# A two-block transformer kernel on one core: roots of the first mixing by logarithms, seven banks for projections, another order for down banks and condition sums

## The chip, the cores and the metric

One core of one Trainium2 chip runs the whole program in one launch. The metric is device microseconds of one execution. The engines are TensorE (PE; its weight loads, PEld, overlap its matmuls), VectorE (DVE), ScalarE (ACT), GpSimd (POOL) and SyncE (SP, which here only issues DMAs). Each works through its own queue in order; semaphores tie them together.

## The reference

512 tokens of width 1024 go through a first block and then two layers of a second block, all in float32.

```python
# first block: three kinds of attention, a gated merge, a squared-relu MLP
aq, ak, bq, bk, cq, ksel, kwin = (rms_norm(...) per head of 64, with a gain)
oa = rms_norm(diff_attention(aq, ak, av, lam), subln) * 0.8          # att_a: two maps, p0 - lam * p1
ob = banded_attention(bq, bk, bv, window 128, sinks)                  # att_b
oc = nsa_attention(cq, compressed, selected, window; sigmoid gates)   # att_c
x = x + sum_n(sigmoid(mg_n) * (branch_n @ w_branch_n)) @ w_out
x = x + square(relu(rms_norm(x) @ w_up)) @ w_down
# each of two layers: mod = silu(c) @ w_ada + b_ada gives 9 vectors of 1024 (shift, scale, gate x 3)
x = x + 0.5 * gate0 * swiglu(modulate(rms_norm(x)))                   # width 2816
x = x + gate1 * mixer(modulate(rms_norm(x)))                          # chunked attention, pooling, forgetting attention
x = x + 0.5 * gate2 * swiglu(modulate(rms_norm(x)))
```

## The kernel before

**Matmuls.** Activations lie with features on partitions and the 512 tokens in the free dimension, as chunks of 128 features. Each float32 matmul of a projection is three in the faster fp32r form: high x high, high x low, low x high (L1536 to L1538). A *group* is one output tile of 128 features x 512 tokens: 8 chunks x 3 matmuls, in one bank of PSUM out of eight. POOL splits each weight piece of 512 KB into its high and low part (L1489, L1492) ahead of PE. In the feed-forward parts pairs of output tiles are computed as a *set* of 7 products per side with half-size operands (`new_set`, L942; matmuls L1605 to L1607). A product is 12 matmuls of 256 columns; the products come in the order P1, P2, P5, P6, P7, P3, P4, each for the gate side and then for the up side. P1 writes into `banks[1]` and P2 into `banks[0]` of its side, from `SET_BANKS`: ((6, 2), (7, 3)) or ((6, 4), (7, 5)). A set's first sums (L2112, L2114 on DVE) use banks 0 and 1, which hold silu(c) until the last condition sum has read them; ACT moves the weights there first (L1787).

**Queues.** `plan` (L1148) writes out one list of steps, and every engine walks through it, taking the steps that are its own; so the order of steps fixes the order of each queue. `HELD` notes for each bank which semaphore frees it, and `take(bank)` puts that wait ahead of the next writer. A group takes the next bank of its *ring*, a tuple of banks; `RING_AT` keeps the position per ring, also across stages. `late(step, quanta)` postpones a step by so many quanta of two chunks; `passed` gives out at most one per quantum.

**Roots.** Every normed projection (and each of the four outputs of att_a, "differential") needs 1/sqrt of a mean. `new_root` puts: ACT squares the bank (L1829); two quanta later PE sums over partitions into bank 4 (L1630); then there are two ways. With `logs` false, ACT takes a Sqrt (L1839) and DVE the reciprocal in two halves (L2162), at the third and fourth quantum. With `logs` true, ACT does Identity with scale and bias, Ln, Exp with -0.5, and a Square into the other buffer, for which it waits for the output of the root before (L1843 to L1850); DVE makes a correction step of two products (L2153, L2157). Both end in the output product (L2178, or L2172 with L2175 for att_a), which frees the group's bank. Before the change the layers' second projections (inside att_a2) use logarithms and all other roots a Sqrt.

**Tables.** ACT's functions come in table sets. A load (ACT_TABLE_LOAD) is put by the compiler ahead of an activation whose function the present set lacks. `put("tables")` loads the set with logarithm and exponential by hand.

**Attention.** `attend` gives four beats per *duo* (one or two blocks of queries of a pair of heads): turn and scores, exponentials, products with V, scaling of probabilities. `weave` puts the stage's dense groups between the beats. Scores use banks 0 and 1, transposes 2 and 3, sums 4, outputs 5. DVE takes minima (L2204) and inverses (L2218); in att_a it also joins the two maps (L2236), behind ACT's scaling (L1885), and only then are the score banks free. The first mixing has 12 duos in att_a with 13 dense groups, 16 in att_b with 4 groups and the compression.

**Condition sums.** `mod` is 144 rows of 1024 products, as 72 loads of 1 MB (issued by ACT) and 72 sums of two rows each on DVE (L2297), nine in each of eight runs of eight down groups (`with_ada`). A down group's result is added to x on DVE (L2458), which frees its bank. `ada_sum` steps stand ahead of the group that they are given to, and each issues the load two ahead.

Of the kernel before, what the change touches and what calls it, by code (L numbers as in the profile page):

```python
# [12 lines left out]
S = 512  # L13
# [16 lines left out]
ADA_PART = 9  # L30
# [19 lines left out]


SCORE_BANKS, T_BANKS, SUM_BANK, O_BANK = (0, 1), (2, 3), 4, 5
BARE_RING = (5, 6, 7)
MIX_RINGS = dict(att_a=(3, 6, 7), att_b=(3, 6, 7), att_c=(6, 7), att_a2=(6, 7), att_c2=(6, 7))
UP_FIRST = (6, 7, 4)
MIX_FIRST, MIX_RING = (6, 7, 5), (0, 1, 3)
UP_RING, DOWN_RING, DOWN_FOUR = (0, 1, 2, 3), (4, 5), (6, 7, 4, 5)
FFN_FIRST = (6, 7, 4, 5)


# [10 lines left out]
TOTAL = {}  # L71
# [14 lines left out]
def put(*step):  # L86
    ORDER.append(step)
# [89 lines left out]
def late(step, quanta=1):  # L177
    LATER.append([quanta, step])
# [27 lines left out]
def run_all(jobs):  # L206
    for _ in stretches(jobs):
        pass
# [36 lines left out]
def new_root(what, gain, dest, src, logs=False):  # L245
    q = Root(what, gain, dest, src, tick("qk_squared"), logs)
    for name in ("qk_summed", "qk_rooted", "qk_out"):
        assert tick(name) == q.n
    if logs:
        q.squares = tick("qk_squares")  # L250
    else:
        q.inverses = tick("qk_inverse", PARTS)
    put("qsq", q)

    def total():
        q.sum_before = take(SUM_BANK)
        HELD[SUM_BANK] = ("qk_rooted", q.n)
        put("qsum", q)

    def inverse(part):  # L260
        put("qinv", q, part)
        if part < PARTS - 1:
            return
        put("qfin", q)
        ROOTED[0] = q.n
        if what == "differential":
            tick("br_hi")
            q.out = tick("br_lo")
            HELD[SUM_BANK] = READY[("br_a", dest[1])] = ("br_lo", q.out)

    late(total, 2)
    for part in range(PARTS):
        late(lambda part=part: inverse(part), 3 + part)
    return q
# [150 lines left out]
def norm_rest(m, firsts):  # L425

    if m.halves == WHOLE:
        norm_sum(m, -1)
        put("prep1")
        put("prep2")  # L430
        load_bias(0, 0)
        load_bias(1, 0)
        norm_spread(m, -1)
        for c in norm_chunks(m, -1):
            for g in firsts:
                mm(g, c, c + 1)
        return

    second = norm_chunks(m, 1)
    for c in range(KC):  # L440
        for g in firsts:
            mm(g, c, c + 1, 0)
        next(m.first, None)
        if c == 1:
            norm_sum(m, 1)
        if c == 3:
            norm_spread(m, 1)
        if c >= 4:
            next(second)
    sums = quarter_sums(m) if len(m.which) == 2 and m.quartered else iter(())  # L450
    for c in range(KC):
        for g in firsts:
            mm(g, c, c + 1, 1)
        if next(second, None) is None:
            next(sums, None)
    for _ in sums:
        pass
# [159 lines left out]
def attend(chain, kind):  # L617
# [39 lines left out]
    def products(j):  # L657
        if 0 <= j:
            u = duos[j]
            kind = u.kind  # L660
            if u.first:
                u.o_before = take(O_BANK)
            u.need_v = READY[V_AT[kind]]
            put("pv", u)
        if 0 <= j and duos[j].last:
            u = duos[j]
            if kind == "att_a":
                HELD[O_BANK] = ("oa_copied", tick("oa_copied"))
                new_root("differential", ("small", "subln", 0), ("r0", u.pair), u)
            else:  # L670
                u.out = tick("br_hi")
                assert tick("br_lo") == u.out
                HELD[O_BANK] = READY[(OUT_AT[kind], u.pair)] = ("br_lo", u.out)
                put("bhigh", u)
        for e in list(masks):
            e[0] -= 1
            if e[0] == 0:
                masks.remove(e)
                mask_bias(e[1])
# [25 lines left out]
    out = []  # L705
# [21 lines left out]
def compress(ring):  # L727


    def after(g):  # L730
        assert tick("cmp_gelu") == 1 and tick("cmp_turned") == 1 and tick("cmp_copied") == 1
        put("cgelu", g)
        HELD[g.bank] = ("cmp_copied", 1)
        late(lambda: put("cturn", g))
        late(out)

    def pieces():
        return [new_piece(("cmp", kv, m), KC * P, split=False) for m in range(4) for kv in (0, 1)]

    def gather(kv):  # L740
        for j in range(CMP_STRIDE):
            READY[("cmp_x", j)] = ("cmp_gathered", 2)
        tick("cmp_gathered")
        put("cgather", kv)

    def out():
        at = RING_AT[ring]
        RING_AT[ring] = at + 1
        g = Group("cmpo", 1, "", ring, P, None, None, bank=ring[at % len(ring)])
        g.before = take(g.bank)  # L750
        for name in ("cmp_out", "cmp_sq", "vc_done", "cmp_sum", "cmp_inv", "cmp_root", "kc_done"):
            tick(name)
        HELD[g.bank] = ("kc_done", 1)
        put("cout", g)

        def rest():
            g.done = take(SUM_BANK)
            HELD[SUM_BANK] = ("cmp_inv", 1)
            put("ckey", g)
        late(rest)  # L760

    return gather, Group("cmph", CMP_STRIDE, "cmp_x", ring, 2 * P, pieces, after)


# [101 lines left out]
def ada_sum(stop):  # L866
    m = tick("ada_used") - 1
    put("adasum", m, TOTAL["c_made"])
    for b in SUM_BANKS:
        HELD[b] = ("ada_used", m + 1)  # L870
    if ADA_AT[0] < stop:
        ada_load()
    l, n = divmod(m + 1, ADA_ALL)
    if n == ADA_FIRST:
        put("coef", l, 0)
    elif n == 0:
        put("coef", l - 1, 1)
        put("coef", l - 1, 2)


def with_ada(groups, stop):

    def condition():
        tick("c_made")
        put("cond", [take(b) for b in SUM_BANKS], TOTAL["cond_loaded"])
    out = [condition]
    for i, g in enumerate(groups):
        out += [lambda: ada_sum(stop)] * sum(6 * k // ADA_PART == i for k in range(ADA_PART)) + [g]
    return out


# [256 lines left out]
def plan():  # L1148
    put("prep")
    tick("first_loaded", 32)  # L1150
    tick("prep_loaded", 32)
    tick("late_loaded", 48)
    tick("constants")
    tick("lam_sums", 2)
    tick("lam_exps")
    m = new_norm(("mix",), *MIX_NORM, WHOLE)
    for c in range(KC):
        READY[("x", c)] = (f"x_loaded{c}", tick(f"x_loaded{c}", 16))
        norm_square(m, c)
    q = [normed(("aq", i), "query", ("small", "gain", 0), ("r0", i)) for i in range(4)]  # L1160
    k = [normed(("ak", i), "key", ("small", "gain", 1), ("r0", 4 + i)) for i in range(4)]
    order = [q[0], k[0], q[1], k[1], q[2], k[2], q[3], k[3]]
    norm_rest(m, by_halves(order[:2]))
    put("signs")
    mask_bias(0)
    mask_bias(1)
    run_all(order[2:] + [lambda: put("lam")] + token_groups(("av",), S, "v0"))
    flush()

    ring = MIX_RINGS["att_a"]  # L1170
    b = [normed(("bq", i), "query", ("small", "gain", 2), ("r1", i), ring) for i in range(4)]
    ks = [normed(("bk",), "key", ("small", "gain", 3), ("k5", 0), ring),
          normed(("ck", 2), "key", ("small", "gain", 6), ("k5", 1), ring),
          normed(("ck", 4), "key", ("small", "gain", 7), ("k5", 2), ring),
          plain(("ck", 0), ("k5", 3), ring), plain(("ck", 1), ("k5", 4), ring)]
    tick("gate_tanh")
    chain = chain_of(("att_a", "att_b"), 0)
    weave(chain, "att_a", [ks[0]] + b + ks[1:] + token_groups(("vbc",), V_BC, "v_bc", ring)
          + [lambda: put("gates", TOTAL["plain_out"])])

    ring = MIX_RINGS["att_b"]
    cq = [normed(("cq", i), "query", ("small", "gain", 4), ("r2", i), ring) for i in range(4)]
    gather, hidden = compress(ring)
    weave(chain, "att_b", [lambda: gather(0), cq[0], lambda: gather(1), cq[1], hidden, cq[2], cq[3]])
    ring = MIX_RINGS["att_c"]
    weave(chain_of(("att_c",), 0), "att_c", merge((0, 0), "br_a", "set", ring) + merge((0, 1), "br_b", "mid", ring))
    tick("cond_loaded", 16)
    put("condload")
    run_all(merge((0, 2), "br_c", "last"))
    flush()  # L1190
    m = new_norm(("mlp",), *FFN_NORM)
    close([("wo", 0, d) for d in range(KC)], KC, "m", "half", m)
    m = mlp(m)
    for l in range(2):
        m = layer(l, m)
# [1425 lines left out]
```

How the kernel before makes its waits and increments, by code:

```python
    def wait_ge(self, name, n):  # L1244
        if n > self.seen.get(name, 0):
            self.e.wait_ge(self.sem[name], n)
            self.seen[name] = n
# [1 line left out]
    def wait_at(self, at):  # L1249
        if at:
            self.wait_ge(*at)
# [1 line left out]
    def settle(self):  # L1253
        self.n += 1
        self.e.wait_ge(self.sem[self.chain], self.n)
# [189 lines left out]
        @block.sync  # L1446
        def _(sp):
            E = Engine(sp, sem, "out_done")
            for c in range(0, KC, 2):
                sp.dma_start(x[:, c, :], x_in[:, c, :]).then_inc(sem[f"x_loaded{c}"], 16)
            for p, piece in enumerate(PIECES):
                if p >= NR:
                    former = PIECES[p - NR]
                    if not former.pair:
                        E.wait_ge("w_used", former.used + 1)
                    else:
                        E.wait_at(former.pair.ops["P4" if former.second else "P2"].low)
                        E.wait_at(summed(former.pair, "S4"))
                src = weights[AT[p] - piece.cols * P:AT[p]].rearrange("(p n) -> p n", p=P)
                sp.dma_start(raw[:, p % NR, 0:piece.cols], src).then_inc(sem[f"loaded{p % NR}"], 16)
            for d in range(KC):
                E.wait_ge("x_added", TOTAL["x_added"] - KC + d + 1)
                sp.dma_start(out[:, d, :], x[:, d, :]).then_inc(sem["out_done"], 16)
            sp.wait_ge(sem["out_done"], 16 * KC)
# [145 lines left out]
            def norm_sum(m, half):  # L1610
                E.wait_ge("n_added", m.squares[KC - 1, half][0])
                for b in blocks(half):
```

## Time and profile before

| | us |
|---|---|
| median of 3 runs | 3424.58 (3424.27 to 3425.43) |
| the profiled execution, its own time | 3431.12 |
| its span | 3429.2 |
| mean granted clock of PE | 0.989 |
| busy in the span: PE, PEld, DVE, ACT, POOL | 3322.7, 2840.7, 1701.2, 1329.7, 2104.7 |

Stages in the profiled execution: norm and projections of the first mixing to 98.8 us, att_a and att_b to about 325, att_c and the merge to about 600, the MLP to about 1000, layer 0 to about 2220 and layer 1 to the end. The eight runs of down groups with sums end at 813, 901, 1127, 1255, 1986, 2115, 2342 and 2478 us. In a row of the profile "x" is a count, a number in brackets with an arrow is the engine's idle time ahead of an instruction and what ended it, and PEclk is the granted share of the full 2.4 GHz clock of PE (the other level is 1.2 GHz).

### The profile page before, as it was taken

What the parts mean: (1) busy time and instruction counts of PE and PEld (TensorE: products, weight loads), DVE (VectorE), ACT (ScalarE), POOL (GpSimd) and SP (SyncE); (2) the same over time, 40 slices, a digit from 0 to 9 for tenths busy, and PEclk for the clock granted to TensorE, in tenths of its full rate; (3) what the DMA queues carried; (4) which work ended last, traced back from release to release, by engine and by line L of the source; (5) the groups of instructions that cost most, each with busy time, mean ns of one, the idle gap of its engine ahead of it and who ended that gap; (6) DMA issues with size and microseconds to landing.
All of it is one profiled execution on the core that took longest, in us unless ns stands there. A gap on an engine that the chain in (4) does not pass through costs nothing.

```text
span 3429.2 us, 50538 instructions
## 1 busy us (share of the span) xinstructions
PE 3322.7 (97%) x19962; PEld 2840.7 (83%) x19962; DVE 1701.2 (50%) x3322; ACT 1329.7 (39%) x2793; POOL 2104.7 (61%) x1242
## 2 busy tenths in 40 slices
PE   7888999999999999999999999999999999999999
PEld 6665778988899999667789999998997677789998
DVE  6454332465646665452224667566755432236444
ACT  2566651322233533354313353443342543224333
POOL 7425548676676467645676646764675656785565
PEclk9989999999999999999999999999999999999999
DMA  4122223235425452222232545244522222232232
GB/s 145 63 68 91 71 69 113 92 124 206 177 92 188 141 187 86 86 64 83 87 105 97 188 147 184 87 153 179 188 96 72 77 73 82 87 103 100 98 105 81
DMA packets 108267, 388.60 MB, mean 113 GB/s; under 512 B 12400, under 2 KB 12784, under 8 KB 98816
## 3 DMA queue, kind: packets, MB, share of 16 engines
q1 hardware_dynamic: 88272, 292.76, 25.6%
q10 hardware_dynamic: 19760, 92.62, 7.5%
q8 instruction: 159, 2.61, 0.3%
q14 instruction: 76, 0.62, 0.1%
HBM read 383.20 MB, written 2.13 MB: 112 GB/s over the span
## 4 chain that ended last, share of the span: by engine, by line
PE 83%; DVE 7%; DMA 4%; ACT 3%; POOL 1%; issue 1%; ACTq 0%; DVEq 0%; POOLq 0%
PE psum L1536 18%; PE psum L1537 17%; PE psum L1538 17%; PE psum L1605 7%; PE psum L1607 7%; PE psum L1606 7%; DMA ada_t<-ada_dram 4%; PE psum L1647 2%; PE psum L1697 2%; DVE ada_t L2297 2%; PE psum L1670 2%; PE psum L1630 1%; DVE rs_t L2162 1%; POOL w_lo L1492 1%; POOL w_hi L1489 1%
## 5 line engine op out<-in xcount | busy, mean ns | idle before, releaser
L1489 POOL TENSOR_TENSOR w_hi<-raw,ones 128x1024 fp32r<-128x1024 f32 (+2 forms) x437 | 747.8, 1711 | 642.0 <-PE psum L1538 634.2
L1492 POOL TENSOR_TENSOR w_lo<-raw,w_hi 128x1024 fp32r<-128x1024 f32 (+2 forms) x437 | 944.3, 2161 | 34.2
L1504 POOL TENSOR_TENSOR w_hi<-raw,w_hi 128x512 fp32r<-128x512 f32 x312 | 403.6, 1308 | 556.1 <-ACT w_hi L1801 551.6
L1536 PE MATMUL psum<-h_hi,w_hi 128*128 128x512 f32 (+2 forms) x1704 | 659.1, 387 | 23.4 <-DVE r L2178 10.9
L1538 PE MATMUL psum<-h_hi,w_lo 128*128 128x512 f32 (+2 forms) x1704 | 626.7, 368 | 0.0
L1537 PE MATMUL psum<-h_lo,w_hi 128*128 128x512 f32 (+2 forms) x1704 | 626.5, 368 | 0.0
L1536 PEld LDWEIGHTS psum<-h_hi,w_hi 128*128 128x128 f32 (+1 forms) x1704 | 324.4, 190 | 103.1 <-issue 30.7
L1536 PE MATMUL psum<-a_hi,w_hi 128*128 128x512 f32 (+1 forms) x1064 | 392.6, 369 | 0.0
L1537 PE MATMUL psum<-a_lo,w_hi 128*128 128x512 f32 (+1 forms) x1064 | 392.0, 368 | 0.0
L1538 PE MATMUL psum<-a_hi,w_lo 128*128 128x512 f32 (+1 forms) x1064 | 391.8, 368 | 0.0
L1537 PEld LDWEIGHTS psum<-h_lo,w_hi 128*128 128x128 f32 (+1 forms) x1704 | 324.5, 190 | 56.0 <-issue 9.5
L1538 PEld LDWEIGHTS psum<-h_hi,w_lo 128*128 128x128 f32 (+1 forms) x1704 | 323.6, 190 | 55.5
L1605 PE MATMUL psum<-t_hi,w_hi 128*128 128x256 f32 x1248 | 353.2, 283 | 0.0
L1606 PE MATMUL psum<-t_lo,w_hi 128*128 128x256 f32 x1248 | 353.2, 283 | 0.0
L1607 PE MATMUL psum<-t_hi,w_hi 128*128 128x256 f32 x1248 | 353.2, 283 | 0.0
L1801 ACT ACTIVATE w_hi<-raw 128x512 fp32r<-128x512 f32 x312 | 192.1, 626 | 377.5 <-DVE mod_raw L2297 236.7
L1605 PE MATMUL psum<-h_hi,w_hi 128*128 128x256 f32 x936 | 267.9, 286 | 24.1 <-DVE x L2458 24.1
L1606 PE MATMUL psum<-h_lo,w_hi 128*128 128x256 f32 x936 | 266.9, 285 | 0.0
L1607 PE MATMUL psum<-h_hi,w_hi 128*128 128x256 f32 x936 | 266.8, 285 | 0.0
L1605 PEld LDWEIGHTS psum<-t_hi,w_hi 128*128 128x128 f32 x1248 | 239.6, 192 | 0.0
L1606 PEld LDWEIGHTS psum<-t_lo,w_hi 128*128 128x128 f32 x1248 | 239.6, 192 | 0.0
L1607 PEld LDWEIGHTS psum<-t_hi,w_hi 128*128 128x128 f32 x1248 | 239.6, 192 | 0.0
(230 smaller groups left out, 6146.8 us busy)
## 6 DMA issues: line engine op xcount, KB each, us to landing
raw<-weights_dram SPq DMA_DIRECT2D x487, 512.0 KB, 3.5
ada_t<-ada_dram ACTq DMA_DIRECT2D x72, 1024.0 KB, 6.6
raw<-weights_dram SPq DMA_DIRECT2D x76, 256.0 KB, 2.6
raw<-weights_dram SPq DMA_DIRECT2D x32, 384.0 KB, 3.6
bias_t<-biases_dram ACTq DMA_DIRECT2D x36, 256.0 KB, 2.9
bias_t<-cum_dram ACTq DMA_DIRECT2D x16, 256.0 KB, 3.4
out_dram<-x SPq DMA_DIRECT2D x8, 256.0 KB, 2.0
raw<-weights_dram SPq DMA_DIRECT2D x4, 408.0 KB, 3.2
```

The lines of the kernel that those rows point to most:

```text
L1489: nc.gpsimd.tensor_tensor(high, piece, ones[:, 0:1].to_broadcast([P, n]), ALU.mult)\
L1492: nc.gpsimd.tensor_tensor(w_lo[:, p % NR, 0:n], piece, high.bitcast(F32), ALU.subtract)\
L1504: nc.gpsimd.tensor_tensor(low_of(op), src, high_of(op).bitcast(F32), ALU.subtract)\
L1536: mm(dst, lh, rh, start=first, stop=False)
L1537: mm(dst, lh, rl, start=False, stop=False)
L1538: return mm(dst, ll, rh, start=False, stop=last)
L1605: mm(dst, wh[:, w], hi, start=start, stop=False, skip_group_check=True)
L1606: mm(dst, wh[:, w], lo, start=False, stop=False, skip_group_check=True)
L1607: ins = mm(dst, wl[:, w], hi, start=False, stop=stop, skip_group_check=True)
L1647: ins = mm(scores_at(u, p, half), q, k, start=p.column == 0, stop=u.kind != "att_c2", skip_group_check=True)
L1670: ins = nc.tensor.transpose(psum[0:rows, t:t + P], s[:, c:c + rows], ident)
L1801: fn(high_of(op), src, ACT.Copy).then_inc(sem["high_act"], 1)
```

## The change

Three things. (1) The 15 roots of the first mixing from att_a on (7 normed keys and queries, 4 differential, 4 of att_b) use the logarithm form; the table set with logarithm and exponential is loaded by hand ahead of att_a, and again behind the gates' Tanh, behind gelu and behind the compressed key's Sqrt. (2) Projections take seven banks in turn where they took three: from the third group on in the first mixing (`FIRST_RING`), from the fourth on in the layers (`MIX_RING`). (3) The nine condition sums of a run are spread over seven of its eight groups (2, 1, 1, 2, 1, 1, 1, 0 ahead of each) where they were over six (2, 1, 2, 1, 2, 1, 0, 0), and down groups take banks in the order 4, 5, 6, 7 where it was 6, 7, 4, 5.

```diff
@@ constants @@
-BARE_RING = (5, 6, 7)
+BARE_RING, FIRST_RING = (5, 6, 7), (7, 0, 1, 3, 2, 5, 6)
-MIX_FIRST, MIX_RING = (6, 7, 5), (0, 1, 3)
-UP_RING, DOWN_RING, DOWN_FOUR = (0, 1, 2, 3), (4, 5), (6, 7, 4, 5)
+MIX_FIRST, MIX_RING = (6, 7, 5), (0, 1, 3, 2, 6, 7, 5)
+UP_RING, DOWN_RING, DOWN_FOUR = (0, 1, 2, 3), (4, 5), (4, 5, 6, 7)
@@ attend, products @@
-                new_root("differential", ("small", "subln", 0), ("r0", u.pair), u)
+                new_root("differential", ("small", "subln", 0), ("r0", u.pair), u, True)
@@ compress, after gelu and after the key @@
         put("cgelu", g)
+        put("tables")
...
             put("ckey", g)
+            put("tables")
@@ with_ada @@
-        out += [lambda: ada_sum(stop)] * sum(6 * k // ADA_PART == i for k in range(ADA_PART)) + [g]
+        out += [lambda: ada_sum(stop)] * sum(7 * k // ADA_PART == i for k in range(ADA_PART)) + [g]
@@ plan @@
+    for g in order[2:]:
+        g.ring = FIRST_RING
...
-    run_all(order[2:] + [lambda: put("lam")] + token_groups(("av",), S, "v0"))
+    run_all(order[2:] + [lambda: put("lam")] + token_groups(("av",), S, "v0", FIRST_RING))
...
-    b = [normed(("bq", i), "query", ("small", "gain", 2), ("r1", i), ring) for i in range(4)]
+    b = [normed(("bq", i), "query", ("small", "gain", 2), ("r1", i), ring, True) for i in range(4)]
(the same for bk, ck 2, ck 4 and cq)
...
     tick("gate_tanh")
+    put("tables")
...
-          + [lambda: put("gates", TOTAL["plain_out"])])
+          + [lambda: (put("gates", TOTAL["plain_out"]), put("tables"))])
```

## Rows read from the trace of the kernel before

**Rows 1.** The page, its first part: busy time, share, instructions.
```profile
PE 3322.7 (97%) x19962; PEld 2840.7 (83%) x19962; DVE 1701.2 (50%) x3322; ACT 1329.7 (39%) x2793; POOL 2104.7 (61%) x1242
```
**Rows 2.** Windows: length, busy time of each engine, PEclk, DMA share, GB/s.
```profile
38.00:46.00 8.00, 5.71 (x17) 3.76 (x16) 3.41 (x3) 0.93 (x2) 7.84 (x5) 0.79 0.20 66
98.00:325.00 227.00, 189.84 (x974) 134.60 (x973) 123.17 (x308) 144.76 (x314) 87.78 (x63) 0.92 0.23 75
900.00:920.00 20.00, 14.13 (x93) 13.44 (x92) 14.35 (x24) 7.97 (x17) 3.86 (x3) 0.83 0.19 64
1388.00:1402.00 14.00, 10.43 (x30) 7.00 (x29) 8.14 (x7) 1.98 (x3) 7.82 (x4) 0.76 0.01 2
1440.00:1560.00 120.00, 116.28 (x624) 82.28 (x623) 54.72 (x145) 68.40 (x146) 61.71 (x32) 0.99 0.23 71
2340.00:2360.00 20.00, 11.50 (x66) 10.53 (x65) 15.15 (x24) 6.98 (x13) 5.06 (x4) 0.74 0.57 210
3360.00:3380.00 20.00, 20.00 (x169) 20.00 (x169) 13.91 (x23) 12.57 (x26) 10.22 (x8) 1.00 0.24 79
```
**Rows 3.** Groups of instructions by form, 98 to 325 us, DVE and ACT.
```profile
L2162 DVE RECIPROCAL rs_t<-rs_t 128x256 f32<-128x256 f32 x30 | 51.4, 1734 | 23.3 <-ACT rs_t L1839 23.3
...
L1869 ACT ACT_TABLE_LOAD x17 | 21.8, 1283 | 0.3
L1839 ACT ACT_TABLE_LOAD x14 | 18.0, 1283 | 1.2 <-issue 1.0
```
**Rows 4.** Timeline of a root by logarithms in layer 0: start, duration, instruction.
```profile
1441.57 1.02 PE L1630 MATMUL psum<-sq_t,cst 128*128 128x512 f32 x2
...
1444.61 0.63 ACT L1850 ACTIVATE rs_t<-rs_t 128x512 f32<-128x512 f32 x1
1445.38 0.69 DVE L2153 SCALAR_TENSOR_TENSOR psum<-psum,rs_t 128x512 f32<-128x512 f32 x1
...
1446.84 0.75 DVE L2178 SCALAR_TENSOR_TENSOR r<-psum,lay,rs_t 128x512 f32<-128x512 f32 x1
```
**Rows 5.** Timeline of a root by Sqrt in att_a: its sum and output.
```profile
108.11 1.02 PE L1630 MATMUL psum<-sq_t,cst 128*128 128x512 f32 x2
...
113.29 0.75 DVE L2178 SCALAR_TENSOR_TENSOR k<-psum,small,rs_t 128x512 f32<-128x512 f32 x1
```
**Rows 6.** Waits, 98 to 325 us: total, times, longest.
```profile
PE psum L1647 <- DVE s_sb L2236: 16.1, 10, 3.2
...
PE psum L1697 <- ACT pt_sb L1902: 8.9, 10, 1.8
```
**Rows 7.** Timeline of ACT in att_a: a Sqrt ahead of a scaling.
```profile
178.97 0.69 ACT L1839 ACTIVATE rs_t<-psum,eps_t 128x512 f32<-128x512 f32 x1
```
**Rows 8.** Timeline of ACT at the start of att_a.
```profile
98.92 0.60 ACT L1857 ACTIVATE v<-psum 128x512 f32<-128x512 f32 x1 [4.84 <-PE psum L1538]
99.54 1.28 ACT L1869 ACT_TABLE_LOAD   x1
100.83 0.40 ACT L1869 ACTIVATE s_sb<-s_sb,row_min 128x128 f32<-128x128 f32 x1
```
**Rows 9.** Timeline of PE in the projections of two mixings.
```profile
41.50 0.53 PE L1536 MATMUL psum<-h_hi,w_hi 128*128 128x512 f32 x1 [2.29 <-DVE r L2178]
...
1394.21 0.79 PE L1536 MATMUL psum<-h_hi,w_hi 128*128 128x512 f32 x1 [3.57 <-DVE r L2178]
```
**Rows 10.** Waits of PE in the whole span, and PE's timeline at 2350 us.
```profile
PE psum L1605 <- DVE x L2458: 24.1, 10, 8.1
...
2350.47 0.55 PE L1605 MATMUL psum<-h_hi,w_hi 128*128 128x256 f32 x1 [8.09 <-DVE x L2458]
```
**Rows 11.** Timeline of DVE at the end of the seventh run of sums.
```profile
2344.24 1.22 DVE L2297 CUSTOM_DVE_ANT_0 ada_t<-ada_t,psum 128x1024 f32<-128x1024 f32 x1 [1.38 <-DMA ada_t<-ada_dram]
...
2349.58 0.74 DVE L2458 SCALAR_TENSOR_TENSOR x<-psum,res,x 128x512 f32<-128x512 f32 x1
...
2352.89 0.74 DVE L2458 SCALAR_TENSOR_TENSOR x<-psum,res,x 128x512 f32<-128x512 f32 x1
```

More of the change, by code:

```diff
@@ L1166, in plan @@
     mask_bias(1)
-    run_all(order[2:] + [lambda: put("lam")] + token_groups(("av",), S, "v0"))
+    run_all(order[2:] + [lambda: put("lam")] + token_groups(("av",), S, "v0", FIRST_RING))
     flush()
     ring = MIX_RINGS["att_a"]
-    b = [normed(("bq", i), "query", ("small", "gain", 2), ("r1", i), ring) for i in range(4)]
-    ks = [normed(("bk",), "key", ("small", "gain", 3), ("k5", 0), ring),
-          normed(("ck", 2), "key", ("small", "gain", 6), ("k5", 1), ring),
-          normed(("ck", 4), "key", ("small", "gain", 7), ("k5", 2), ring),
+    b = [normed(("bq", i), "query", ("small", "gain", 2), ("r1", i), ring, True) for i in range(4)]
+    ks = [normed(("bk",), "key", ("small", "gain", 3), ("k5", 0), ring, True),
+          normed(("ck", 2), "key", ("small", "gain", 6), ("k5", 1), ring, True),
+          normed(("ck", 4), "key", ("small", "gain", 7), ("k5", 2), ring, True),
           plain(("ck", 0), ("k5", 3), ring), plain(("ck", 1), ("k5", 4), ring)]
     tick("gate_tanh")
+    put("tables")
     chain = chain_of(("att_a", "att_b"), 0)
     weave(chain, "att_a", [ks[0]] + b + ks[1:] + token_groups(("vbc",), V_BC, "v_bc", ring)
-          + [lambda: put("gates", TOTAL["plain_out"])])
+          + [lambda: (put("gates", TOTAL["plain_out"]), put("tables"))])
     ring = MIX_RINGS["att_b"]
-    cq = [normed(("cq", i), "query", ("small", "gain", 4), ("r2", i), ring) for i in range(4)]
+    cq = [normed(("cq", i), "query", ("small", "gain", 4), ("r2", i), ring, True) for i in range(4)]
     gather, hidden = compress(ring)
```

## The prediction

> **What bounds the kernel now.** I read the page first: TensorE is busy for 3322.7 us, 97% of the span, so only time in which TensorE stands, or runs at half clock, can be won or lost; no part of the change removes a matmul [rows 1]. Then I cut the span in windows of 20 us and kept those in which PE is not busy throughout or its clock is under 1.00. They fall in three kinds of place, and the change has one part for each.
>
> First mixing, att_a and att_b: PE is busy 189.84 of 227 us at a granted clock of 0.92 [rows 2]. Idle is 37.2 us. The clock knows two levels, 2.4 and 1.2 GHz; a mean of 0.92 over 227 us means up to 18 us lost to the lower one. Projections of a mixing: PE is busy 5.71 of 8 us at 0.79 in the first mixing and 10.43 of 14 us at 0.76 in layer 0 [rows 2], with one clear stall in each. Starts of a set of products behind down groups with condition sums: PE 14.13 and 11.50 of 20 us at 0.83 and 0.74 at the two worst [rows 2].
>
> **Part 1, roots by logarithms (15 roots in the first mixing).** Before, a root is a Sqrt on ACT and two reciprocal halves on DVE; after, ACT does four activations (Identity, Ln, Exp, Square) and DVE two short products. Both forms are in this trace, because the layers already use logarithms.
> - DVE: the 30 halves take 51.4 us [rows 3], 3.43 a root. After: two products of 0.69, from 1445.38 to the start of the output product at 1446.84, 1.46 [rows 4]. Saved 1.97 a root, 30 us of DVE.
> - ACT tables: 17 + 14 loads of 1.283 us stand in the stretch [rows 3], with one each for gelu and the compressed key's Sqrt on top. After: one at the start, and two each (in and back) for the gates' Tanh, gelu and that Sqrt, so 7. Saved 26 x 1.283 = 33.4 us of ACT.
> - ACT work after the sum: Square ends at 1445.24, the sum at 1442.59, so 2.65 us [rows 4]; a Sqrt alone takes 0.69 [rows 7]. Added 15 x 1.96 = 29.4 us. ACT's load is thus about even: -4 us.
> - Latency: the sum of a root ends at 109.13 and its product out at 114.04, 4.9 us [rows 5]. With logarithms and nothing in between it is 2.65 + 1.46 + 0.75 = 4.9 [rows 4]. No gain on a bare root: the reciprocals' time moves from DVE to ACT.
>
> So 30 us off DVE buys little by itself. What can be won are waits in which a reciprocal or a table load is in the way of attention. The scores wait for the probabilities made on DVE (L2236) for 16.1 us in 10 waits; the products with V wait 8.9 us for an ACT copy, and ACT gets no lighter [rows 6]. Going through the cycles of scores one by one: where the sum ends just ahead of the scaling of probabilities (L1885), only the Sqrt of 0.69 (at 178.97) lies between, its table having been loaded while ACT waited [rows 7]; there 2.65 puts the scaling up to 1.96 later. I count two such, +3.1. Where reciprocal halves delay the minima, or a load of 1.28 lies uncovered, 1 to 1.7 us are won: four such in the differential part, -5.8, and four roots behind it at about 1, -4. The two loads around the gates' Tanh sit ahead of a copy that PE needs: +2. Sum -4.7. Two stalls over 3 us then become shorter, and one drop of the clock may go with them (the 18 us are shared by the five drops that windows of 10 us show, 3.6 each, part of it idle): I take -2.3. **Part 1: -7.** Bounds: all of the 16.1 and a half of the clock's 18, -25; and +29.4 if each root's longer ACT part is always in the way. I lean to the near end because layer 0's attention, with logarithms, has PE busy 116.28 of 120 us at 0.99 [rows 2], though it has more matmuls to cover a wait.
>
> The Trainium skill (ScalarE: Activation LUTs, What ACT_TABLE_LOAD costs) gives 1.28 us for the load and 1.38 more for a drain, 2.66 a switch. By that page 26 fewer switches would free 36 us more of ACT, and I estimate that the part would then be worth some 20 us. The trace has the load from 99.54 to 100.82 and the next activation at 100.83 [rows 8]: no drain is seen, and the sum goes by 1.283.
>
> **Part 2, seven banks for projections.** With three banks the fourth group of a run waits until the root of the first is written out of its bank. PE idles 2.29 us ahead of 41.50 and 3.57 ahead of 1394.21, both for L2178 [rows 9]; the second layer repeats the latter. Behind each the clock falls: 0.76 over 14 us is 3.4 us lost, of which some 0.35 lies in the idle time; 0.79 over 8 us is 1.7 [rows 2]. Sum 2.29 + 1.7 + 2 x (3.57 + 3.05) = 17.2. With seven banks a bank comes back seven groups later, at over 5 us a group, against the 4.9 of a root. What is late next? POOL's splits, 4.33 us a piece against PE's 5 and over: not. The price: in the first mixing and in layer 0 the ring now puts the last groups of V into banks 0 and 1, and the first scores must wait for the copy (0.60 at 98.92 [rows 8], and its signals): 2 x 0.7. In layer 1 the ring has moved on by two, and the banks are free. 17.2 - 1.4: **part 2: -16.** Bounds -18 and -10, should the clock fall at another stall instead.
>
> **Part 3, condition sums over seven groups, down ring (4, 5, 6, 7).** Eight runs of down groups carry nine sums each. In the five of them whose next set has its first products in banks 4 and 5, PE waits: 24.1 us in 10 waits; the longest, 8.09, ends at 2350.47 [rows 10]. These banks belong to down groups 6 and 7, whose additions end at 2350.3 and 2353.6 on DVE, behind the ninth sum, which waited 1.38 us for its megabyte from 2342.86 on and ended at 2346.5, and behind the set's own sums [rows 11]. The sums are paced by DMA (a sum about every 5 us), so their times stay when they are spread over seven groups. But banks 4 and 5 now belong to groups 4 and 5, whose additions come after the seventh and eighth sum, the later at 2342.86 (what ends there now is the addition behind the eighth sum): the first two products, 12 matmuls each, at the 169 in 20 us of a stretch of sets [rows 2] 1.42 us each, run at once. Then the third waits for bank 6, the fourth for bank 7, whose additions come only some 0.6 us sooner than now (one addition fewer ahead of them). Left here: 4.6 + 1.8 us. By the same reckoning I get 4.2 left at 900, 0.6 each at 1130 and 1990, 0 at 815: 11.8. So 24.1 - 11.8 = 12.3 less idle. Clock: 0.83 and 0.74 over 20 us are 3.4 and 5.2 us lost, of which some 2.4 lie in idle time and 6.2 in work; 2.5 I leave at 2345. 12.3 + 3.7: **part 3: -16.** The other three runs have banks 2 and 3 first and gain nothing; there banks 6 and 7 are now freed late, but the fourth product starts 4.3 us behind the down groups and the last addition ends about 4.1 behind: 0, at worst 0.5 each. Bounds -25 (no wait left) and -6 (the sums slip by a group, 5 us, at two places).
>
> Sum: -7 - 16 - 16 = -39. Against the profiled execution's own 3431.1 us that is 3392.1. It lies 6.5 us above the median of the runs, 3424.6, so the median becomes **3386**.
>
> **The rivals.**
> 1. Reciprocals were the real brake: part 1 gives -25. For: 15 roots had 4.9 to 11 us from sum to output, so DVE's queue does pile up. Against: equal bare latency. Time 3425 - 57 = 3368. Chance 0.20. (The Trainium skill's page on ScalarE, by its drain, points here too.)
> 2. ACT becomes the bound of the first mixing: part 1 gives +10 (five roots more than I counted lie ahead of a scaling of probabilities). For: the Sqrt at 178.97 [rows 7] and its like. Time 3403. Chance 0.18.
> 3. The wait moves whole from banks 4 and 5 to 6 and 7, part 3 gives -6: 3396. For: sums by DMA, additions 6 and 7 in the same place. Against: two products do run in between. Chance 0.12. That the spread over seven does nothing by itself is part of my forecast.
> 4. Slower: every root's Square and its wait for the previous root's output hold up ACT, 2.65 us on the path 15 times, each with a stall near 3 us behind which the clock falls for some 3 us. At 2.1 us a root it takes back parts 2 and 3, from 2.6 on the kernel is slower; at 3.2, 48 - 32 = +16, 3441. Against: layer 0's attention at 116.28 of 120 us [rows 2]. Chance 0.05; and 0.05 that it ends within 0.2%.
>
> My forecast has 0.40. It reaches with its neighbours from 3360 to 3411, which leaves out rival 4 and the far half of rival 1. By 0.2% (6.8 us, what a measurement here can tell): faster 0.90, same 0.05, slower 0.05.
>
> **What would show it.** No idle row for L2178 in the three projections and clock 1.00 there; some 12 us of L1605 waiting for L2458 in place of 24.1, the long ones behind two products; no L2162 in att_a and att_b, 7 loads in the stretch, and PE's idle time for L2236 still near 12 of 16. Wrong if those waits vanish altogether (rival 1), or if PE waits more for L1885's outputs.

## The result, and the profile after

The changed kernel takes 3388.78 us (median of 4 runs, 3386.66 to 3393.18) against 3424.43 for the kernel before (4 runs, 3420.85 to 3425.43): ratio 0.990, interval [0.988, 0.992], 35.6 us less. Forecast were 3386 and 39 us less. The profiled execution after took 3389.5 us of its own (span 3387.7), before 3431.1. The two traces thus lie 41.6 us apart; some 6 of these are luck, since the execution profiled before was slower than the median of its kernel by 6.7 us.

The page, its first part, and the windows of the changed kernel, moved with the work so that they answer to [rows 1] and [rows 2] (34 to 42 answers to 38 to 46, 93 to 320 to 98 to 325, and so on; 1112 to 1132 is new):

```profile
span 3387.7 us, 50581 instructions
PE 3305.3 (98%) x19962; PEld 2830.7 (84%) x19962; DVE 1674.4 (49%) x3322; ACT 1323.0 (39%) x2813; POOL 2102.6 (62%) x1242
```

```profile
34.00:42.00 8.00, 8.00 (x33) 5.91 (x32) 4.92 (x4) 1.98 (x3) 7.84 (x5) 1.00 0.33 123
93.00:320.00 227.00, 190.51 (x989) 134.61 (x988) 98.06 (x322) 140.72 (x340) 89.34 (x65) 0.93 0.24 77
888.00:908.00 20.00, 16.88 (x122) 15.79 (x121) 15.84 (x25) 8.76 (x19) 5.25 (x5) 1.00 0.28 103
1112.00:1132.00 20.00, 16.33 (x111) 15.69 (x110) 14.35 (x23) 9.86 (x20) 6.40 (x5) 0.83 0.45 175
1367.00:1381.00 14.00, 14.00 (x57) 10.50 (x57) 11.89 (x10) 3.64 (x6) 13.76 (x8) 1.00 0.22 74
2314.00:2334.00 20.00, 17.83 (x126) 16.55 (x125) 14.80 (x25) 9.23 (x20) 6.70 (x6) 1.00 0.61 229
```

PE is busy for 17.4 us less than before [rows 1] with the same 19962 matmuls; that part is the clock's. The other 24.1 us of the 41.5 between the two spans are idle time that is gone. The forecast, added up in the same way, had 25.0 us of idle time and 13.8 of clock.

Both projection windows are full, at a clock of 1.00: PE ran 57 matmuls in 14 us where it ran 30. The two starts of a set went from 93 to 122 matmuls in 20 us and from 66 to 126. Att_a and att_b have 15 more matmuls in 227 us, with 25 us less DVE and 4 us less ACT.

The waits of PE in 93 to 320 us, and the one that stood first in the whole span ([rows 6, 10] before: 16.1, 8.9 and 24.1):

```profile
PE psum L1652 <- DVE s_sb L2241: 15.8, 10, 4.1
PE psum L1702 <- ACT pt_sb L1907: 7.6, 7, 2.1
PE psum L1541 <- POOL w_lo L1497: 3.4, 1, 3.4
```

```profile
PE psum L1610 <- DVE x L2463: 10.6, 7, 3.3
```

**A ledger of the two profiled executions.** Both have 19962 matmuls, so one can ask when the same matmul, counted from the start, began in each. The lead of the changed kernel grows by 1.0 us ahead of the first projections; 3.6 in them (to the first scores, 98.8 before, 94.2 after); 3.4 in att_a and att_b (part 1's place); in the projections of the two layers 6.7 and 6.5. The five starts of a set that part 3 aims at give +2.3, +5.2, -2.1, +2.5 and +8.6, in sum 16.4. The rest is some 4 us net: 1.9 for a wait for the merge (below), and 1.6 each for stretches at the lower clock from 1502.7 and 2724.7 us on in the execution before, which the one after does not have, less 0.9 for the first scores of layer 0, which wait for V; what is left is small and of both signs. Such a ledger says where these two executions differ, and not yet what the edits did; for that the traces of the single parts are needed (below).

### The profile page after: what moved, and what is told of

It is laid out like the page before. It is cut to its first block, busy times and chain, and to the rows that moved or that the text cites. A ratio compares the mean times of both kernels' runs of the same rounds, so it can differ in the third digit from the quotient of the medians.

```text
span 3387.7 us, 50581 instructions
## 1 busy us (share of the span) xinstructions
PE 3305.3 (98%) x19962; PEld 2830.7 (84%) x19962; DVE 1674.4 (49%) x3322; ACT 1323.0 (39%) x2813; POOL 2102.6 (62%) x1242
## 4 chain that ended last, share of the span: by engine, by line
PE 86%; DVE 5%; DMA 4%; ACT 3%; POOL 1%; issue 1%; ACTq 0%; DVEq 0%; POOLq 0%
PE psum L1541 19%; PE psum L1542 18%; PE psum L1543 18%; PE psum L1610 7%; PE psum L1612 7%; PE psum L1611 7%; DMA ada_t<-ada_dram 3%; PE psum L1652 2%; PE psum L1702 2%; PE psum L1675 2%; DVE ada_t L2302 1%; PE psum L1635 1%; POOL w_lo L1497 1%; POOL w_hi L1494 1%; DVE x L2463 0%
## 5 line engine op out<-in xcount | busy, mean ns | idle before, releaser
L1497 POOL TENSOR_TENSOR w_lo<-raw,w_hi 128x1024 fp32r<-128x1024 f32 (+2 forms) x437 | 943.9, 2160 | 34.3
L1610 PE MATMUL psum<-h_hi,w_hi 128*128 128x256 f32 x936 | 266.6, 285 | 10.6 <-DVE x L2463 10.6
```

The costliest lines, as they stand in the source:

```text
L1497: nc.gpsimd.tensor_tensor(w_lo[:, p % NR, 0:n], piece, high.bitcast(F32), ALU.subtract)\
L1610: mm(dst, wh[:, w], hi, start=start, stop=False, skip_group_check=True)
```

## The experiments

Each run was timed beside the kernel before on the same chip; a ratio below is to that kernel. Its medians beside the four batches of runs were 3426.3, 3421.7, 3427.9 and 3425.1 us.

**Each part alone.** The edits are those of the change, one part at a time; the fourth run has only the `7 * k // ADA_PART` of part 3.

> The kernel before with the logarithms for the 15 roots of the first mixing alone, and nothing else of the change. My prediction's part 1 says -7 us against before (about 3417). The two traces set side by side give the stretch of att_a and att_b -3.5 us, which a clock drop of its own could have masked. Rival 1 (the reciprocals were the real brake) says -25 (3400), rival 2 (ACT is the bound) +10 (3434). Each root's output should again come 4.9 us behind its sum where nothing lies between, and the three stalls of the projections and of the condition's sums should stay as before.

> The kernel before with the rings of seven banks alone. Prediction: -16 us (3409): 2.3 + 1.7 us in the first mixing, 3.6 + 3.05 in each layer, less 2 x 0.7 for first scores that wait for V. From the two traces I now expect the gain in the places themselves to be 4.2 and 2 x 6.5, the price 2 x 0.9. The bound on the other side, -10, would show if the clock fell at another stall in place of the one removed.

> The kernel before with the condition's sums over seven down groups and the ring 4, 5, 6, 7. Prediction: -16 us (3409), the largest piece at 2345 us (about -8.5) and the next at 900 (about -5); PE's waits for the additions 24.1 us before, 12 after. Rival 3 (the wait moves whole to banks 6 and 7): -6 (3419). In the trace of the changed kernel one place, the third run of sums, came out 2 us worse.

> The kernel before with the condition's sums over seven groups in place of six, the ring left at 6, 7, 4, 5. My prediction gives the spread nothing by itself, since the sums are paced by their loads: 0 us, within 2. If the sums are paced by their place in DVE's queue instead, the additions of groups 6 and 7 come later by up to 5 us a run, and the kernel is slower by 5 to 10; if the earlier additions come sooner and free TensorE earlier, it is faster by as much.

| run | ratio, interval | us against before | forecast |
|---|---|---|---|
| part 1 | 0.9976 [0.9960, 0.9992] | -8 | -7 |
| part 2 | 0.9960 [0.9943, 0.9976] | -14 | -16 |
| part 3 | 0.9947 [0.9928, 0.9965] | -18 | -16 |
| the spread alone | 0.9988 [0.9971, 1.0005] | -4, not told from 0 | 0 |

The third column is the ratio times the median before; the differences of the medians are -5, -13, -16 and -8 us. By the ratios the three parts sum to -40, by the medians to -34; together they gave -36. All three terms are right within their intervals (some 6 us to either side), and the spread by itself shows nothing that can be measured, though 4 us can't be excluded. The ring alone, with the sums over six groups, was not run.

The traces show the places. PE's waits for the additions are 14.8 us in 8 with part 3 alone and 23.3 in 10 with the spread alone. With part 1 alone the stalls of the projections stood as before (10.9 us for the roots' outputs in the whole span).

How far the waits for the additions differ from one execution to the next shows when all kernels are set side by side, with the lead over the trace before counted at the same matmuls:

| kernel | waits for the additions, us | the longest of them near 2345 us | lead gained at the five starts |
|---|---|---|---|
| before | 24.1 | 8.1 | |
| part 1 alone | 19.8 | 4.0 | +2.9 |
| part 2 alone | 24.4 | 1.6 | -2.5 |
| the spread alone | 23.3 | 5.0 | -2.5 |
| part 3 alone | 14.8 | 2.7 | +9.6 |
| changed | 10.6 | 1.6 | +16.4 |
| changed, second profile | 6.7 | none | +26.2 |

The kernels with part 1 or part 2 alone have no edit at the sums, and yet the wait of 8.09 us [rows 10] is 4.0 and 1.6 us in them: half of it and more was bad luck of the execution before. Over all five starts the kernels with part 3 stand apart from those without it, so that the part works is shown; how its gain is shared among the places is not.

One stall of the projections teaches something about the clock. PE's timeline and a window of the kernel with part 1 alone, at the place of [rows 9]:

```profile
40.44 0.50 PE L1539 MATMUL psum<-h_hi,w_hi 128*128 128x512 f32 x1 [2.28 <-DVE r L2181]
```

```profile
36.00:46.00 10.00, 7.72 (x32) 5.69 (x31) 6.39 (x5) 1.42 (x3) 9.84 (x5) 1.00 0.16 54
```

The same stall of 2.3 us, and the clock stayed at 1.00, where the trace before has 0.79 [rows 2]. The traces of part 3 alone and of the spread alone have this stall too and no drop behind it. Behind the stalls of 3.6 us in the two layers the stretch at the lower clock is 3.4 us long in four of these eight cases and 6.8 in the other four. So whether a drop follows such a stall, and how long it is, differs between executions. Stalls behind condition sums differ themselves. The kernel with part 2 alone, which changes nothing there, ran at 0.57 from 813 to 821 us, where the trace before has no drop; but PE had waited longer ahead of it, 3.67 us where it was 0.19 (at 813.20):

```profile
812.39 0.35 PE L1607 MATMUL psum<-h_hi,w_hi 128*128 128x256 f32 x1 [3.67 <-DVE x L2460]
```

The records of PE's clock hold 12 stretches at the lower level before, 75 us in all, and 8 after, 38 us.

**The changed kernel again, beside three variants of it.**

> The changed kernel once more, beside three variants of it on one chip. The first measurement gave 0.990 of the kernel before; the three parts alone gave -8, -14 and -18 us by their ratios, -40 in all. If the parts add up the ratio is 0.988 to 0.990; if the parts alone had luck with drops of the clock it is above 0.991.

It came to 3388.5 us (6 runs, 3383.2 to 3395.4), ratio 0.9903 [0.9887, 0.9919].

*Another order of the seven banks.* The edit, with q, k and V of layer l taking `MIX_RINGS_V[l]`:

```diff
-BARE_RING, FIRST_RING = (5, 6, 7), (7, 0, 1, 3, 2, 5, 6)
+BARE_RING, FIRST_RING = (5, 6, 7), (7, 3, 2, 0, 1, 5, 6)
-MIX_FIRST, MIX_RING = (6, 7, 5), (0, 1, 3, 2, 6, 7, 5)
+MIX_FIRST, MIX_RINGS_V = (6, 7, 5), ((3, 2, 0, 1, 6, 7, 5), (3, 2, 1, 0, 6, 7, 5))
```

> The changed kernel with the seven banks of the projections in another order, so that the last groups of V lie in banks 7, 3 and 2 and not in 0 and 1, which the first scores need. My prediction priced that wait at 2 x 0.7 us; the traces show 1.2 to 1.3 us ahead of the first scores at 93 and 1415. Expected: no idle row ahead of the first scores for a copy of V, and 2 us less than the changed kernel (within 1 to 3). If another copy is just as late (queries or keys in T's banks), 0.

It took 3382.5 us (4 runs), ratio 0.9889 [0.9872, 0.9906]. The wait is gone. The first scores of att_a, in the changed kernel and in this one:

```profile
94.24 1.14 PE L1652 MATMUL psum<-r 64*128 64x128 f32 x8 [0.78 <-ACT v L1862]
```

```profile
93.85 1.14 PE L1652 MATMUL psum<-r 64*128 64x128 f32 x8
```

Counted by matmuls, it leads the changed kernel by 0.8 us more behind each of the two places, 1.6 in sum. That is what the expectation had (1 to 3). Of the 6 us between the medians the rest can't be told from scatter: the intervals overlap.

*Loads in halves.* The first half of a megabyte is asked for as soon as the first of a sum's two instructions has read its old content:

```diff
-                        E.wait_ge("ada_used", m - 1)
+                        E.wait_ge("ada_first", m - 1)
-                    act.dma_start(ada_t[:, m % 2, :, :], ada[m].rearrange("p (a n) -> p a n", a=ADA))\
-                        .then_inc(sem[f"ada_loaded{m % 2}"], 16)
+                    act.dma_start(ada_t[:, m % 2, 0, :], halves[:, 0, :]).then_inc(sem[f"ada_early{m % 2}"], 16)
+                    if m >= 2:
+                        E.wait_ge("ada_used", m - 1)
+                    act.dma_start(ada_t[:, m % 2, 1, :], halves[:, 1, :]).then_inc(sem[f"ada_loaded{m % 2}"], 16)
```

On DVE each of the two instructions waits for its half.

> The changed kernel with each megabyte of the condition's matrix loaded as two halves, the first half asked for as soon as the first of a sum's two instructions on DVE is done. It tests that the nine sums of a run are paced by the round trip of their loads (as my prediction of part 3 says) and not by DVE's queue. If so a sum comes 0.5 to 1.2 us sooner each, the last one some 5 us sooner, the waits left at the second, third, fifth and seventh run (about 16 us in the trace of the changed kernel) shrink by half, and the kernel is 6 to 10 us faster than the changed one. If DVE's queue or ACT's queue is the pace: 0. If the second issue on ACT costs more than it gives: up to 5 us slower.

It took 3377.1 us (4 runs, 3375.6 to 3378.8), ratio 0.9868 [0.9850, 0.9887]: 11 us under the changed kernel (expected 6 to 10), with no run of the one inside the range of the other. The waits of DVE for these loads in the whole span, in the changed kernel and in this one:

```profile
DVE ada_t L2302 <- DMA ada_t<-ada_dram: 102.1, 49, 4.9
```

```profile
DVE ada_t L2307 <- DMA ada_t<-ada_dram: 65.2, 59, 4.1
```

PE's waits for an addition at the start of a set are no longer among its waits; the windows at the second, third and seventh run of sums are full:

```profile
880.00:900.00 20.00, 20.00 (x117) 17.70 (x116) 16.53 (x26) 7.01 (x13) 5.24 (x5) 1.00 0.58 212
1105.00:1125.00 20.00, 20.00 (x147) 19.05 (x146) 11.28 (x17) 10.03 (x20) 7.03 (x6) 1.00 0.49 161
2305.00:2325.00 20.00, 20.00 (x150) 19.18 (x149) 10.90 (x17) 9.12 (x19) 7.43 (x7) 1.00 0.47 160
```

That the sums are paced by the round trip of their loads is shown: had DVE's or ACT's queue set the pace, this edit would have given nothing. The Trainium skill (DMA: Bandwidth & Descriptors, Bandwidth) has the rule to batch DMAs to 1 MiB or more for their rate. Here two of 512 KB beat one of 1024 KB: what counts is when a buffer may be filled again.

*DVE's load given back.* Four reciprocals of 128 columns behind the output of each of the 15 roots:

```diff
+            def fill():
+                for k in range(4):
+                    v.reciprocal(mod_raw[:, :, 0:64], cst[:, P:2 * P].rearrange("p (a n) -> p a n", a=2)).then_inc(sem["dve_chain"], 1)
+                    E.settle()
```

> The changed kernel with four reciprocals of 128 columns put on DVE behind the output of each of the 15 roots of the first mixing, into a buffer that is written anew later. It gives DVE back about the load that the logarithms took off it (3.4 us a root), without lengthening the root. My theory, that only a few cycles gain by the logarithms, says +3 to +7 us in att_a and att_b, at most what part 1 brought. If DVE's load was the real brake (rival 1) the cost is 15 or more; if DVE has slack there, 0.

It took 3438.3 us, ratio 1.0057 [1.0036, 1.0078]: 50 us over the changed kernel, for 15 x 3.91 = 59 us of fill. My own theory (+3 to +7) fell, and the line of rival 1 (15 or more) is met. But the fill is not the load that was taken away, as the expectation had it. It is 59 us in blocks of 3.9 behind the output, where the logarithms took off 31 us net (the reciprocals' 51.4, less 20.7 for the products), and the real edit gave 8 us and not 25. DVE's timeline in this kernel:

```profile
123.36 0.70 DVE L2158 SCALAR_TENSOR_TENSOR psum<-psum,rs_t 128x512 f32<-128x512 f32 x1 [5.30 <-ACT rs_t L1855]
124.09 0.69 DVE L2162 SCALAR_TENSOR_TENSOR rs_t<-psum,rs_t 128x512 f32<-128x512 f32 x1
124.82 0.75 DVE L2189 SCALAR_TENSOR_TENSOR r<-psum,small,rs_t 128x512 f32<-128x512 f32 x1
125.49 3.91 DVE L2171 RECIPROCAL mod_raw<-cst 128x128 f32<-128x128 f32 x4
129.43 0.23 DVE L2231 RECIPROCAL row_inv<-row_sum 128x1 f32<-128x1 f32 x2
```

The root's work, and so the fill, stands ahead of the row sums' reciprocal, from which the probabilities are scaled; so it is for 8 of the 15 blocks. PE's waits for the probabilities rose from 15.8 to 35.1 us. The 50 us have two parts. Between the same matmuls, from the first scores to the end of att_b, PE's idle time rose by 33 us, from 35.7 to 69.0. The other 17 go with the clock: the time at its lower level rose there from 31 to 78 us. So DVE is busy for 43% of this stretch in the changed kernel, and yet blocks of 3.9 us put at this place of its queue cost 0.56 of themselves in idle time of PE, and 0.85 with the clock. What a smaller block costs was not measured.

**Where then did the 25 us of DVE go?** The same cycle in the changed kernel, DVE and ACT:

```profile
123.83 0.08 DVE L2209 DVE_READ_ACCUMULATOR2_ANT row_min<- 128x1 f32 x1
128.09 0.70 DVE L2158 SCALAR_TENSOR_TENSOR psum<-psum,rs_t 128x512 f32<-128x512 f32 x1 [4.18 <-ACT rs_t L1855]
128.82 0.41 DVE L2223 RECIPROCAL row_inv<-row_sum 128x1 f32<-128x1 f32 x2
```

```profile
125.44 0.66 ACT L1848 ACTIVATE psum<-psum,eps_t 128x512 f32<-128x512 f32 x1 [2.79 <-PE psum L1635]
127.43 0.63 ACT L1855 ACTIVATE rs_t<-rs_t 128x512 f32<-128x512 f32 x1
127.97 0.49 ACT L1874 ACTIVATE s_sb<-s_sb,row_min 128x256 f32<-128x256 f32 x1
```

The minima are there at 123.9. ACT stands for the root's sum until 125.44, does the four activations, and only then, at 127.97, the first exponential. DVE stands 4.18 us for the root, with the row sums' reciprocal behind it. In this cycle ACT is what comes last: its second exponential ends at 128.9, DVE's first product at 128.8. The group of that first product shows the sum over the stretch; before, the like wait was 23.3 us [rows 3]:

```profile
L2158 DVE SCALAR_TENSOR_TENSOR psum<-psum,rs_t 128x512 f32<-128x512 f32 x15 | 10.4, 695 | 40.4 <-ACT rs_t L1855 40.4
```

So of the 25 us that DVE is less busy between these windows (31 by the roots' own groups; the window after holds 15 more matmuls and their work) 17 came back as a wait at the same place in its queue. The root takes as long as before, and the attention's next step stands behind it on both engines.

**The root behind the scaling.** If that is so, moving the root's work behind the scaling of the same cycle should free PE. First both edits that paid were put together, then DVE's part of the roots (products and output) was moved behind the scaling wherever it stood between the exponentials and the scaling of a cycle (`combo_dve`), then ACT's four activations too (`combo_both`), and last both for roots 9 to 11 alone (`combo_three`). The core of the edit, on the order of steps:

```diff
+    roots = [s[1] for s in ORDER if s[0] == "qsum" and s[1].logs and s[1].n <= 23]
...
+        moved = [ORDER[i] for i in at]
+        moved.insert(0, ("qroot", q))
...
+        ORDER[:end] = rest[:put_at] + moved + rest[put_at:]
```

> The changed kernel with both edits that measured well: the order of the seven banks (V away from banks 0 and 1) and the condition's loads in halves. Expected: the two lie in different places and add up: 11 us of the half loads and 1.7 of the bank order, 12 to 13 us under the changed kernel, about 0.986 of the kernel before. If the bank order's 6 us of the first measurement were real and not scatter of the clock, 0.985.

> The former kernel, and on DVE alone the two products and the output of each logarithm root of the first mixing that stood between the exponentials and the scaling of the same cycle of scores are put behind that scaling (11 roots or so). It tests where the 30 us that part 1 took off DVE went: in the trace of the changed kernel DVE stands 40 us in 8 waits at the head of its queue for ACT's four activations, with the reciprocal of the row sums right behind. If those waits hold up the probabilities, PE's waits for them (15.8 us in 10) fall by a third or more and the kernel is 5 to 12 us faster than without this edit. If ACT is what comes last (it does the root ahead of the scaling in its own queue), the wait only changes its name: 0, within 2. If the roots' outputs, now later, are what PE waits for next: slower.

> As the last one, and on ACT too the four activations of those roots stand behind the scaling of the probabilities. If ACT's queue is the second half of the same wait, this one is 5 to 15 us faster than the kernel without either move, and PE's waits for the probabilities fall to half or less of 15.8 us. If the roots' outputs then come too late for the banks of the projections (three in att_a and att_b) and for the next scores, PE waits for the root's output or for the sum in place of it, and the gain is lost or turned round.

> The kernel with the bank order and the half loads, and of the last edit only what paid: the first three of the 15 roots (9, 10 and 11) have their four activations and their DVE work behind the scaling of the probabilities; the others stay where they were. With all of them moved PE's four waits for the probabilities from 110.97 to 140.28 us (2.18, 0.70, 1.01 and 1.95) were gone and a matmul at 140.5 came 7.7 us sooner, then 6.3 us were lost in one wait of the next root's sum for the differential output. Expected: the four waits gone, that long wait back at about 2.2, and 5 to 8 us less than the kernel without the edit (3366, 0.982 of the kernel before). If the stalls only move to the cycle of the differential root, 0.

| run | median us | ratio, interval |
|---|---|---|
| combo | 3373.4 | 0.9843 [0.9828, 0.9858] |
| combo_dve | 3380.0 | 0.9860 [0.9845, 0.9875] |
| combo_both | 3380.4 | 0.9860 [0.9843, 0.9876] |
| combo_three | 3371.6 | 0.9844 [0.9827, 0.9860] |

The two edits add up: 15 us under the changed kernel by the medians and 20 by the ratios, since the two were not timed side by side (expected 12 to 13, ratio 0.986). No kernel here is better beyond the scatter. Both moves of all the roots made it slower, by 6.6 and 7.0 us against `combo`, timed side by side. If DVE or ACT held up the probabilities I had expected 5 to 12 and 5 to 15 us less; what came true are the other branches of both expectations.

The move on DVE alone shows which engine comes last. DVE hardly stands for the roots any more (4.7 us in one wait, against 36.9 in 8 in `combo`), but it now stands for ACT's exponentials. Its first wait from 90 to 325 us:

```profile
DVE row_inv L2245 <- ACT s_sb L1893: 39.6, 34, 5.7
```

In `combo` this wait is 13.1 us. The wait has changed its name, as the expectation had it for the case that ACT comes last, and PE's waits for the probabilities fell only from 15.7 us in 10 to 12.6 in 7. With ACT's part moved as well they are 8.6 in 4, so ACT's queue is the other half of that wait. What undoes it stands in PE's rows. In combo PE waits 2.18, 0.70, 1.01 and 1.95 us for the probabilities ahead of four scores. PE's rows with an idle time, from 100 to 141 us, in combo:

```profile
110.97 0.70 PE L1654 MATMUL psum<-r 64*128 64x256 f32 x4 [2.18 <-DVE s_sb L2246]
121.93 0.70 PE L1654 MATMUL psum<-r 64*128 64x256 f32 x4 [0.70 <-DVE s_sb L2246]
129.97 1.13 PE L1654 MATMUL psum<-r 64*128 64x512 f32 x4 [1.01 <-DVE s_sb L2246]
140.28 1.14 PE L1654 MATMUL psum<-r 64*128 64x128 f32 x8 [1.95 <-DVE s_sb L2246]
```

In combo_both they are gone, and the matmul at 140.5 us comes 7.7 us sooner (some 1.5 of it because the 3.4 us at the lower clock that combo's execution has from 112.3 us on are missing here). All that is left from 100 to 150 us:

```profile
135.74 1.10 PE L1657 MATMUL psum<-sq_t,ones 128*128 128x512 f32 x2 [0.41 <-DVE rs_t L2187]
138.70 0.68 PE L1714 MATMUL psum<-pt_sb,v 128*128 128x128 f32 x4 [0.47 <-ACT pt_sb L1929]
148.41 2.05 PE L1657 MATMUL psum<-sq_t,cst 128*128 128x512 f32 x2 [6.28 <-DVE br_a L2205]
```

The last of them takes back most of it: by 160 us the lead over combo is 0.2. The differential root's output lies in the sums' one bank, the next root's sum needs that bank, and a differential root that is put off puts off everything behind it (2.18 us in combo, 6.28 here). Farther on the moved roots stand ahead of the next minima on DVE, and PE waits for these:

```profile
239.95 1.23 PE L1674 MATMUL psum<-k,r 64*128 64x256 f32 x4 [4.85 <-DVE row_min L2234]
257.93 0.49 PE L1674 MATMUL psum<-k,r 64*128 64x128 f32 x4 [2.65 <-DVE row_min L2234]
```

At the end of att_b combo_both is 6.3 us behind combo, about what the timed runs show. With the move for the first three roots alone that wait is 1.8 again, the waits of 2.18, 0.70 and 1.01 are gone, that of 1.95 stands, and the profiled execution leads combo by 4.9 us up to 304 us. Some 3 of these are lost just there to a longer stretch at the lower clock. The timed runs show no gain: 1.8 us between medians that were not taken side by side, and the same ratio (0.9844 and 0.9843). I expected 5 to 8. The cycle is no longer held up at three places, but a gain in time is not shown.

## Why the prediction was right, point by point

**Part 3 (-16; measured -18 alone).** 24.1 us of waits were to become 11.8, and became 10.6 (6.7 in the second profile of the changed kernel, 14.8 with part 3 alone). The mechanism held: the first two products run at once, then the third and the fourth wait for banks 6 and 7. The places did not: 2.2 us are left at 2322 where I had 6.4, 3.1 at 897 (forecast 4.2), 1.7 at 1972 (0.6), and 3.7 at 1119 where I had 0.6. The third run even lost 2 us, since its sums ran until 1115.9 us and its last two additions ended at 1119 and 1122. I took the times of the sums from one execution; they hang on loads that land sooner or later. The largest piece, some 8.5 us at 2345, rested on a wait of 8.09 us that is 5.0, 4.0 and 1.6 us in the three kernels without the part's ring; that the sum of the part came out right in spite of this is in part luck. Rival 3 (the wait moves whole, -6) is refuted by the time, whose interval is -25 to -12, and by waits of 14.8, 10.6 and 6.7 us against 19.8 to 24.4 in the kernels without the part's ring.

**Part 2 (-16; measured -14 alone).** No idle row for L2183 is left in the three projections, and the clock there is 1.00. The price of the first scores waiting for V was forecast at 0.7, and is 0.78 at both places. The ledger has 3.6, 6.7 and 6.5 us. The clock's terms (1.7 and 2 x 3.05) were booked as if the drops belonged to these stalls. They come and go: behind the first stall one of four traces has a drop, and behind the other two the stretch at the lower clock is 3.4 or 6.8 us. So the sum was right for the pair of traces and 2 us much for the median, within its interval. Not foreseen was that the last merge shares the ring (5, 6, 7): with fewer groups on it ahead, its banks shift, and a wait of 1.6 us for the merge stands once (at 520.92) where it stood twice (1745.45 and 2967.82). Part 2 alone shows the same.

**Part 1 (-7; measured -8 alone, between -14 and -3).** The size and the loads of the engines came out; how the gain splits into waits and clock did not. The forecast had 4.7 us of waits and 2.3 of clock. Between the same matmuls of att_a and att_b PE's idle time is 37.2 us before, 35.7 in the changed kernel and 35.5 both in its second profile and with part 1 alone, so some 1.6 less. With part 2, part 3 and the spread alone, where these roots are the old ones, it is 37.4, 34.3 and 37.0. The time at the lower clock is 34.1 us before and 30.7, 23.9 and 23.9 in the three with the new roots, and 27.3, 34.1 and 34.1 in the others. That part 1 gains is shown by the timed runs; the traces show neither the 4.7 nor the 2.3, and as far as they tell it is luck that the sum came so near. ACT is 4.0 us less busy (forecast 4), seven table loads stand from 94 to 287 us, and the root's bare time is 4.9 us as before (sum to output, 12 of 15 within 2.3 us of that). PE waits 15.8 us in 10 for the probabilities, where I expected it near 12 of 16. In att_a three waits grew by 0.6, 1.1 and 1.8 (forecast +3.1 in two) and three shrank by 1.4, 2.3 and 1.4 (forecast -5.8 in four). One step was wrong in its reason: "30 us off DVE buys little by itself", because a bare root takes as long as before. The fill shows that DVE's time is not free at this place of its queue. The traces point to another reason: 17 us came back as a wait of DVE for ACT's four activations, and where DVE's part of the root was moved away it stood for ACT's exponentials instead. Rival 1 (the reciprocals were the brake, -25) looked at the right queue and is refuted in its price. Rival 2 (ACT as the bound, +10) and rival 4 are refuted by -8. Not named here, and also late, was POOL's split at 279 us: PE waits 3.4 us for it, before 2.0.

Of the drain that the Trainium skill adds to a table load (ScalarE: Activation LUTs, What ACT_TABLE_LOAD costs) the changed kernel shows nothing either. ACT's timeline around the gates' Tanh:

```profile
227.14 1.28 ACT L1985 ACT_TABLE_LOAD   x1
228.44 0.28 ACT L1985 ACTIVATE gates<-v_bc 128x96 f32<-128x96 f32 x1
228.74 1.28 ACT L1952 ACT_TABLE_LOAD   x1
230.03 0.38 ACT L1907 ACTIVATE pt_sb<-psum 128x256 f32<-128x256 f32 x1
```

**The sum.** -39 forecast, -36 measured, and -40 for the parts one by one. The 3 us between lie inside the intervals. That it is as near as this is more than the working could promise: the waits of part 1 were priced at 4.7 us where the traces show some 1.6, the largest piece of part 3 was read from one unlucky execution, and the clock gave 17 us between the two traces where the sum had 14.

## What to carry to other kernels

Before you price work taken off an engine by its busy time, look at what stands behind it in that engine's queue, and whether the new form leaves a wait in the same place: of 25 us of DVE 17 came back as waiting. Before you price a single stall, look for it in a second execution: here one of 8 us was 4.0 and 1.6 us in two kernels that had nothing changed there. Where sums eat loads from two buffers, the round trip of a buffer is the pace, and freeing it in halves can pay though each transfer is smaller. A ring of banks shared by later groups moves those groups too, and a bank handed from one user to the next (the sums' bank here) is what a postponed step collides with.

## What the runs showed that I had not expected

- 59 us of fill on DVE, 8 of its 15 blocks right ahead of a row sums' reciprocal, made the kernel 50 us slower, 33 by idle time of PE and 17 by the clock, with DVE busy for 43% of the changed kernel's stretch.
- The waits of PE behind condition sums came to 19.8, 23.3, 24.1 and 24.4 us in four kernels whose order of banks there is the same, and to 10.6 and 6.7 in two executions of one kernel.
- The clock did not fall behind a stall of 2.28 us in one execution and did behind 2.29 at the same place in another; at the lower level were 75 us of the profiled execution before and 38 after. Single runs of one kernel lie up to 24 us apart (3407 to 3431 for part 1 alone).
- Two loads of 512 KB took 6.5 us each to land, one of 1024 KB 6.4 (medians of the page). The halves are often in flight together, so this is not the time of a half by itself.
